# Gathering the expert inputs of rounds 1 to 7 by products with the selection matrix in place of indirect fetches

## What is computed

```python
hn = rmsnorm(h, g_ffn)
gsel = argmax(hn @ w_rg + b_rg)          # one group of 8 experts for each token
vals, idx = top_k(logits of that group, 2)
for each expert e, for its tokens x:     # 640 pairs of token and expert
    y[token] += weight * ((silu(x @ w_gate[e]) * (x @ w_up[e])) @ w_down[e])
h = h + y;  out = rmsnorm(h, g_final)
```

## Time and profile before

| | before |
|---|---|
| median of 3 runs | 1565.03 us |
| the profiled execution | 1562.23 us |
| its span, first to last instruction | 1560.5 us |
| mean granted TensorE clock | 0.90 |
| PE / PEld busy | 83% / 46% |
| DVE / ACT / POOL busy | 31% / 16% / 6% |
| moved by DMA | 485.52 MB |

### The profile page before, as it was taken

The page is one execution under the profiler, slowest core; times in us unless marked ns, Lnnn a source line. Parts: engine busy times, 40 slices in busy tenths (PEclk is TensorE's granted clock), DMA queues, the critical chain, the costliest instruction groups (busy, mean ns, idle before and its releaser), DMA issues.

```text
span 1560.5 us, 18084 instructions
## 1 busy us (share of the span) xinstructions
PE 1291.7 (83%) x7220; PEld 724.3 (46%) x7220; DVE 477.4 (31%) x1017; ACT 255.0 (16%) x684; POOL 93.6 (6%) x257
## 2 busy tenths in 40 slices
PE   7999999999999998969569668667658758767886
PEld 5667777765578885325125224224214214223232
DVE  4387667233431004313103102202202201211334
ACT  4452332343221111110000000000000000000003
POOL 7800000100010002000000000000000000000000
PEclk9999999999999999879879769869879877887898
DMA  9332233251379653899999999999999999999997
GB/s 216 113 109 88 74 109 103 64 165 55 108 251 389 245 208 114 363 427 428 428 428 427 429 428 429 428 427 427 425 428 426 424 427 418 429 429 421 399 425 314
DMA packets 114181, 485.52 MB, mean 311 GB/s; under 512 B 18325, under 2 KB 86233, under 8 KB 86601
## 3 DMA queue, kind: packets, MB, share of 16 engines
q1 hardware_dynamic: 111496, 475.71, 76.5%
q0 software_dynamic: 2336, 8.94, 1.8%
q10 hardware_dynamic: 288, 0.04, 0.0%
HBM read 477.37 MB, written 10.78 MB: 313 GB/s over the span
## 4 chain that ended last, share of the span: by engine, by line
PE 54%; DMA 41%; DVE 2%; issue 1%; SPq 1%; ACT 1%; POOLq 0%; POOL 0%; ACTq 0%; DVEq 0%
DMA arena<-in_w_up 40%; PE ps L2172 20%; PE ps L2448 12%; PE ps L2236 7%; PE ps L2502 2%; PE ps L2240 2%; PE ps L2107 1%; PE ps L2346 1%; PE ps L2320 1%; PE ps L2042 1%; PE ps L2030 1%; PE ps L2482 1%; SPq L562 1%; DMA arena<-in_x_prompt 1%; PE ps L2094 1%
## 5 line engine op out<-in xcount | busy, mean ns | idle before, releaser
L2448 PE MATMUL ps<-arena 128*32 128x512 f32 x2048 | 320.4, 779 | 204.8 <-DMA arena<-in_w_up 198.2
L2172 PE MATMUL ps<-arena 128*128 128x336 f32 (+1 forms) x1152 | 328.3, 442 | 0.0
L2448 PEld LDWEIGHTS ps<-arena 128*32 128x32 f32 x2048 | 84.7, 138 | 433.5 <-issue 432.8
L2172 PEld LDWEIGHTS ps<-arena 128*128 128x128 f32 x1152 | 215.5, 190 | 95.6 <-issue 3.7
L2502 PE MATMUL ps<-arena 128*32 128x512 f32 x1024 | 146.5, 723 | 20.5 <-DVE arena L1799 20.4
L1787 DVE COPY arena<-ps 128x512 f32<-128x512 f32 x31 | 21.4, 691 | 430.6 <-PE ps L2448 430.6
L1196 ACT ACTIVATE arena<-ps 128x128 f32<-128x128 f32 x32 | 8.8, 276 | 678.6 <-PE ps L2482 678.6
L2236 PE MATMUL ps<-arena 128*128 128x256 f32 x512 | 114.4, 382 | 0.0
L2236 PEld LDWEIGHTS ps<-arena 128*128 128x128 f32 x512 | 96.1, 190 | 14.0 <-issue 1.2
L2502 PEld LDWEIGHTS ps<-arena 128*32 128x32 f32 x1024 | 38.4, 129 | 108.7 <-issue 103.4
L1767 DVE TENSOR_TENSOR arena<-arena,ps 128x1024 f32<-128x1024 f32 (+1 forms) x54 | 65.5, 1218 | 65.4 <-PE ps L2346 50.3
(11 more groups left out here) (405 smaller groups left out, 1005.4 us busy)
## 6 DMA issues: line engine op xcount, KB each, us to landing
arena<-in_w_down SPq DMA_DIRECT2D x61, 2048.0 KB, 22.2
arena<-in_w_gate SPq DMA_DIRECT2D x59, 2048.0 KB, 18.8
arena<-in_w_up SPq DMA_DIRECT2D x59, 2048.0 KB, 23.2
arena<-in_w_in SPq DMA_DIRECT2D x15, 2048.0 KB, 8.9
arena<-in_w_out SPq DMA_DIRECT2D x8, 2048.0 KB, 8.4
arena<-in_w_up SPq DMA_DIRECT2D x10, 1024.0 KB, 15.2
arena<-in_w_gate SPq DMA_DIRECT2D x10, 1024.0 KB, 12.5
arena<-in_w_down SPq DMA_DIRECT2D x6, 1024.0 KB, 19.1
```

What stands on the lines that cost most here:

```text
L2172: mm = te.matmul(o, w, x, start=(k == 0), stop=(k == kt - 1))
L2448: mm = te.matmul(ps[CAP * x:CAP * x + CAP, 0, :], xt[:, 4 * q + at, CAP * i:CAP * i + CAP], (next_first[up] if late and q == 0 else wpiece ...
```

## The change

The fetch of rounds 1 to 7 goes, with what fed it. `gather` now serves these rounds too: each of its four quarters is 12 products (4 column groups x 3 token tiles) into a bank of its own, 2 + i, and the quarters are spread over the experts ahead, each in front of step q of expert i as the two tables give it. `hn` is written by ACT in another order of columns, so that each column group of it is contiguous. `HT` is now made ahead of `x_parts`. The clearing of `xrow` on POOL goes too.

```diff
+GATHER_FIRST = {(2, 2): (0, 1), (3, 0): (2,), (3, 2): (3,)}
+GATHER_AT = {(1, 2): (0,), (2, 0): (1,), (2, 2): (2,), (3, 0): (3,)}
...
@@ gpsimd
-            pool.wait_ge(spread_done, 2)
-            gp.memset(xrow, 0.0).then_inc(xrow_cleared, 1)
-
-            pool.wait_ge(xrow_cleared, 2)
-            for m in range(1, NROUND):
-                pool.wait_ge(row_known, m + 1)
-                pool.wait_ge(rows_loaded, 16 * m)
-                pool.wait_ge(x_turned, 4 * m)
-                pool.indirect_dma_start(out=xrow, out_offset=None, in_=hn_rows,
...
@@ scalar
-                sc.activation(hn[0:TR[t], t, :], hrow[0:TR[t], t, :], ACT.Copy, scale=tok[0:TR[t], t, 1:2])\
-                  .then_inc(hn_ready, 1)
+                sc.activation(hn[0:TR[t], t, :].rearrange("r (k p) -> r p k", k=KT),
+                              hrow[0:TR[t], t, :].rearrange("r (p k) -> r p k", k=KT), ACT.Copy,
+                              scale=tok[0:TR[t], t, 1:2]).then_inc(hn_ready, 1)
...
@@ vector: expert
                 if back:
-                    if ahead is not None:
-                        name_row(ahead)
                     add_part(m - 1, 0)
...
-                if i and inputs is not None:
-                    x_parts(inputs)
                 dve.wait_ge(silu_ready, n + 1)
                 ve.tensor_tensor(HT, Hs, gate_up(i)[:, :, 1, :], ALU.mult)\
                     .then_inc(hid_ready, 1)
+                if i and inputs is not None:
+                    x_parts(inputs)
...
@@ tensor
-            def gather(m):
+            def gather(m, quarters, added):
 
                 pe.wait_ge(p_ready, 3 * (m + 1))
                 pe.wait_ge(hn_ready, 3)
-                pe.wait_ge(xT_a, 2 * m)
-                pe.wait_ge(xT_b, 2 * m)
...
+                if added is None:
+                    pe.wait_ge(spread_copied, 2)
+                else:
+                    pe.wait_ge(sc_added, 6 * added)
+                for i in quarters:
                     for k in range(4):
+                        at = 128 * (4 * i + k)
                         for t in range(3):
-                            mm = te.matmul(ps[:, 2 + i % 2, SLOTS * k:SLOTS * (k + 1)], hn[0:TR[t], t, 4 * i + k:D:KT],
+                            mm = te.matmul(ps[:, 2 + i, SLOTS * k:SLOTS * (k + 1)], hn[0:TR[t], t, at:at + 128],
                                            Psel[0:TR[t], t, :], start=(t == 0), stop=(t == 2))
                     mm.then_inc(x_turned, 1)
...
                 for q in range(4):
                     if start:
                         pe.wait_ge((xT_a, xT_b)[q % 2], q // 2 + 1)
+                    if inputs is not None and first and (i, q) in GATHER_FIRST:
+                        gather(inputs, GATHER_FIRST[i, q], None)
+                    elif inputs is not None and not first and (i, q) in GATHER_AT:
+                        gather(inputs, GATHER_AT[i, q], m)
...
                     if back and q == 1:
-                        if ahead is not None:
-                            name_rows(ahead)
                         add_back(m - 1, 0)
-                        if ahead is not None:
-                            pe.wait_ge(row_known, ahead + 1)
                         add_back(m - 1, 1)
...
                 if back:
                     add_back(m - 1, 2)
                     add_back(m - 1, 3)
-                elif i and inputs is not None:
-                    turn_rows(inputs)
```

More of the change, by code:

```diff
@@ L208, in build @@
         Wh, Wsel = r.take(2, TO), r.take(TO)
-        row_scale, tok = r.take(128), r.take(3, 2)
+        r.take(128)
+        tok = r.take(3, 2)
         r = Region(arena, at_c, 8 * TO)
@@ L1768, in add_part, with expert @@
                     .then_inc(last_added if last else sc_added, 1)
-            def expert(m, i, inputs, ahead=None, sel=None, column=slotp, ending=False):
+            def expert(m, i, inputs, sel=None, column=slotp, ending=False):
                 n, first = EPR * m + i, isinstance(m, int) and m == 0
@@ L1848, in x_parts @@
                     dve.wait_ge(x_turned, 4 * m + i + 1)
-                    ve.tensor_tensor(to[:, 4 * i:4 * i + 4], ps[:, 2 + i % 2, :].rearrange("p (k t) -> p k t", k=4),
+                    ve.tensor_tensor(to[:, 4 * i:4 * i + 4], ps[:, 2 + (i % 2 if first else i), :].rearrange("p (k t) -> p k t", k=4),
                                      bc(gT[:, 4 * i:4 * i + 4].unsqueeze(2), 2, SLOTS), ALU.mult)\
@@ L1863, in select @@
                                             op0=ALU.is_equal, op1=ALU.add).then_inc(p_ready, 1)
-            expert(0, 0, 0, None, 1)
-            expert(0, 1, None, 1)
+            expert(0, 0, 0, 1)
+            expert(0, 1, None)
             expert(0, 2, None)
-            expert(0, 3, 1, None, 2)
+            expert(0, 3, 1, 2)
             dve.wait_ge(hn_ready, 3)
@@ L1871, in _ @@
             with dve.Fori(1, NROUND - 1) as m:
-                expert(m, 0, None, m + 1)
+                expert(m, 0, None)
                 expert(m, 1, None)
                 expert(m, 2, None)
-                expert(m, 3, m + 1, None, m + 2)
+                expert(m, 3, m + 1, m + 2)
             dve.wait_ge(whalf, NROUND - 1)
@@ L1880, in _ @@
                 with dve.Fori(0, NOP) as o:
-                    expert(o + (NROUND - 1), 0, o + NROUND, None, o + (NROUND + 1))
+                    expert(o + (NROUND - 1), 0, o + NROUND, o + (NROUND + 1))
                     for i in range(1, EPR):
@@ L1898, in _ @@
             dve.wait_ge(rconst, 2)
-            expert(m_last, 0, None, None, None, slotq)
+            expert(m_last, 0, None, None, slotq)
             dve.wait_ge(wsel_ready, m_last + 1)
@@ L1913, in _ @@
                                         op0=ALU.is_equal, op1=ALU.add).then_inc(p_ready, 1)
-            expert(m_last, 2, None, None, None, slotp, True)
+            expert(m_last, 2, None, None, slotp, True)
             n = EPR * m_last + (EPR - 1)
@@ L1919, in _ @@
             last_norm(0)
-            dve.wait_ge(rows_named, NROUND + 1)
+            dve.wait_ge(rows_named, 2)
             ve.tensor_copy(wq, ps[:, 1, 1:2]).then_inc(wq_ready, 1)
@@ L2294, in name_first_rows, with turn_rows @@
                 stay_busy(6)
[L2296 to L2307, removed]
+            def turn_rows(quarters):
                 for i in quarters:
-                    if first:
-                        pe.wait_ge(rows_scaled, i + 1)
+                    pe.wait_ge(rows_scaled, i + 1)
                     if i == 2:
-                        pe.wait_ge(xT_a, 2 * m + 1)
+                        pe.wait_ge(xT_a, 1)
                     if i == 3:
-                        pe.wait_ge(xT_b, 2 * m + 1)
+                        pe.wait_ge(xT_b, 1)
                     for k in range(4):
[L2316 to L2320, removed]
+                        mm = te.transpose(ps[:, 2 + i % 2, SLOTS * k:SLOTS * (k + 1)], xrow0[:, 4 * i + k:D:KT], ident)
                     mm.then_inc(x_turned, 1)
@@ L2409, in spread_gains, with expert @@
                               start=True, stop=True).then_inc(gains_spread, 1)
-            def expert(m, i, inputs, ahead=None, turned=None, over=False, ending=False):
+            def expert(m, i, inputs, turned=None, over=False, ending=False):
                 n, first = EPR * m + i, isinstance(m, int) and m == 0
@@ L2421, in expert @@
                     name_first_rows()
-                    turn_rows(0, range(2))
+                    turn_rows(range(2))
                 else:
                     if over and i == 0:
-                        gather(rows)
+                        gather(rows, range(4), m - 1)
                     pe.wait_ge(xT_a, 2 * rows + 2)
@@ L2454, in expert @@
                     if start and q < 2:
-                        turn_rows(0, range(2 + q, 3 + q))
+                        turn_rows(range(2 + q, 3 + q))
                     if back and q == 1:
-                        if ahead is not None:
-                            name_rows(ahead)
                         add_back(m - 1, 0)
-                        if ahead is not None:
-                            pe.wait_ge(row_known, ahead + 1)
                         add_back(m - 1, 1)
@@ L2507, in expert @@
                     spread()
-                    name_rows(ahead)
             expert(0, 0, 0)
-            expert(0, 1, None, 1)
-            expert(0, 2, None)
+            expert(0, 1, None)
+            expert(0, 2, 1)
             expert(0, 3, 1)
@@ L2516, in _ @@
             with pe.Fori(1, NROUND - 1) as m:
-                expert(m, 0, None, m + 1)
-                expert(m, 1, None)
-                expert(m, 2, None)
+                expert(m, 0, None)
+                expert(m, 1, m + 1)
+                expert(m, 2, m + 1)
                 expert(m, 3, m + 1)
@@ L2523, in _ @@
                     for i in range(EPR):
-                        expert(o + (NROUND - 1), i, None, None, o + NROUND, True)
```

(3 more changed lines are left out.)

7 lines of the change are left out of this document (removed).

## The result

| | before | after |
|---|---|---|
| median of the runs | 1563.60 us (1561.61 to 1566.14, 5 runs) | 1554.68 us (1552.31 to 1557.71, 5 runs) |
| profiled execution, its span | 1562.23, 1560.5 | 1554.68, 1552.9 |

The ratio is 0.9944, with a 95% interval of 0.9932 to 0.9956: 8.9 us faster (6.9 to 10.6 by the interval), where 19.0 were forecast.

A forecast was written before the change was run, and what follows sets the result against it. DMA, at its ceiling of about 428 GB/s, was taken as the bound. Gains of 17.5 us (fetches) and 1.5 us (round 7), 19.0 in sum, took the median from 1565.0 to 1546.0 us; range 1541 to 1556.

The forecast's parts named there:

- (1): Fetches of rounds 1 to 7: removing them frees 2.5 us of DMA time each, 17.5 us (10.7 to 18.2).
- Rival B: Fetches: only their bytes count, the extra microsecond each stays; gain 10.7 + 1.5, so 1552.8 us; chance 0.12.
- The guess beside the term: Fetches: time beyond their bytes would fit rows spread unevenly over DMA engines; 2.5 against 1.5 us each.
- (2): PE in each round: quarters of 4.2 us replace old work; 96.9 us busy against DMA's 117.5, all hidden.
- Rival D: PE becomes the bound at 10.9 us per quarter: 70 us slower, some 1635 us; chance 0.06.
- C: PE's longer loop stalls on code at jumps back: up to 12 us, 1558, more likely 1552; chance 0.05.
- the four queued loads cover 19 us: Expert 2 in the rounds: PE comes 1.6 us late, which 19 us of queued loads cover.
- (4): Remaining effects, including round 0's strided `hn` write and reload pushed back 8 to 14 us: priced at nothing.
- my bounds for a quarter: Gather quarter on PE: 2.7 us low, 5.4 at the strided turn's pace, 10.9 at half the clock.
- (3): Expert 3's shorter chain, PE 3 to 6 us earlier: 1.5 us back in round 7 (0 to 2.05).
- The 23 us behind the last load stay: Kernel's end: the time from 1537.77 to 1560.5 us was taken as unchanged.

The follow-up runs named there:

- e6: Kernel before with every indirect fetch of rounds 1 to 7 made twice: 1580.33 us, ratio 1.0111.
- e3: Kernel before without the indirect fetches of rounds 1 to 7, PE multiplying zeros there: 1547.84 us, ratio 0.9896.
- e5: Kernel before with each indirect fetch of rounds 1 to 7 replaced by a plain DMA of 80 rows: 1574.81 us, ratio 1.0075.
- e2: Kernel after with ACT writing `hn` in order and PE reading it with the stride: 1551.41 us, ratio 0.9921.
- e1: Kernel after with round 0's gather moved from expert 2 to expert 3: 1546.13 us, ratio 0.9890.
- e4: Kernel after with six idle products on PE ahead of the wait for `hn` in round 0: 1545.80 us, ratio 0.9884.
- e8: e4 with six more idle products ahead of quarter 2 in each of rounds 1 to 6: 1548.58 us, ratio 0.9906.

## Why the prediction was half right

**(1), the seven fetches at 17.5 us: right.** The intervals are level, e6 measures 2.4 and e3 2.2 to 2.5 per fetch. Rival B, bytes only, falls. The guess beside the term, rows spread unevenly over the engines, is what the packet records fit. By the Trainium skill ("DMA: Bandwidth & Descriptors", the section on the SWDGE path) the term was an estimate of 10.6 us; the runs are against it, and e5 more so.

**(2), PE's work hidden: right in the rounds.** A quarter takes 4.30 us (forecast 4.2), as the timeline of after has it:

```profile
877.48 4.30 PE L2265 MATMUL ps<-arena 128*128 128x128 f32 x24
```

PE's waits for weights fell to 121.8 us in 42 from 177.8 in 43. Rival D falls, and e2 shows that even 7.0 us would have been hidden. C falls too: no stand at the jumps of the longer loop shows in the starts. That agrees with the 2048 instructions of the Trainium skill ("Runtime: NRT & Kernel Launch", on instruction fetch) and not with its window of two pages. Expert 2, put at 28.5 us of PE work, held 24.9, at a granted clock of 0.87 where before stood at 0.7. One sentence of this step was wrong, though, and it is the one the next step leaned on: "the four queued loads cover 19 us".

**(4), "the rest, at nothing": this is the step that failed, by 8.5 us.** It saw the place (the first two quarters in round 0), the cause (ACT's stride, "perhaps double", 11.1 measured) and the reload that is pushed back, and priced it at nothing since the queue there "is full too". Two sizes were off:

- The lateness: "8 to 14 us", measured 19. Against e1, where nothing stands between the steps, PE spends 6.03 + 15.03 + 5.70 = 26.8 us from the end of steps q = 0, 1 to the end of q = 2, 3, instead of 3.54 + 5.34 = 8.9. The quarters alone at 8.4 and ACT's wait gave my 14; half clock in the quarters added 6.5, in steps q = 2, 3 another 2.1 over e4; the wait of 3.5 us that PE had there anyway goes off. The price of half the clock stood in my bounds for a quarter, and I carried it to the rounds and not to this place.
- The cover: "19 us", in truth 11 to 13. SP issues w_gate at 690.88 and w_up at 691.31 behind the same step, so of the four loads ahead of w_up one is late with it. The row of before at 672.24 said so, had I read it: 25.51 us to landing, less two loads of 4.9 for the late pair, less 2.46 for the fetch that goes, leaves 13.2 us. The runs agree: 10.2 us late (682.39, e4) costs nothing, 12.9 late (685.09, e8) leaves 3.0 us of DMA dry. 427 GB/s in slice 18 told the rate of the queue, not its depth.

19 less 13 is 6 us, and the windows lacked 8.5; traffic is back only in the window behind the reload at 691.31, and after entered this stretch some 2 us earlier than before (its w_down loads at 648.36 instead of 650.53), so its queue also ended earlier. Sum: 17.5 - 8.5 = 9.0 against 8.9 measured; that the two agree to 0.1 us is luck, by the interval of 6.9 to 10.6 and by what follows.

**(3), the 1.5 us of round 7: it came out at 0.3, and the end cost 1.4.** Expert 3's chain came out as forecast (under 4 us from step 3 to w_down), and the dip behind the loop's exit is gone. The windows of after there:

```profile
1448.00:1452.00 4.00, 4.00 (x13) 1.23 (x17) 1.69 (x3) 0.28 (x1) 0.00 (x0) 1.00 1.00 426
1452.00:1456.00 4.00, 3.35 (x32) 0.78 (x24) 2.90 (x4) 0.50 (x1) 0.00 (x0) 1.00 1.02 434
```

Yet 1429.11 to 1459.90 is 30.79 us, 1.4 over the pace, and the end got longer. The step of before at 1418.20, the last one ahead of round 7, is this one in after:

```profile
1409.48 5.27 PE L2419 MATMUL ps<-arena 128*32 128x512 f32 x32 [4.75 <-DMA arena<-in_w_up]
```

It comes 8.72 us earlier. The last products of steps q in before and, in the second fence, in after:

```profile
1537.77 1.92 PE L2448 MATMUL ps<-arena 128*32 128x512 f32 x16 [1.53 <-DMA arena<-in_w_up]
```

```profile
1528.78 3.62 PE L2419 MATMUL ps<-arena 128*32 128x512 f32 x16 [3.04 <-DMA arena<-in_w_up]
```

The last load lands 8.99 us earlier, so round 7 gave 0.27 us of the 1.5: it takes 119.30 instead of 119.57 us, and most of the 2.05 above four experts is still paid, without the dip that the step took for its cause. And the span is only 7.6 shorter: behind it 24.1 us pass instead of 22.7, since PE, which waited 3.04 instead of 1.53 us, does this step at half the clock. "The 23 us behind the last load stay" was wrong by 1.4 us, in e1 as well (1520.75 to 1544.9). The 30.79 us I can't explain: DMA stands at 416 to 442 GB/s all through it, so nothing is dry, and e1 has such an interval one expert earlier (1391.66 to 1422.57, 30.91). No run was made for it.

## What to carry to other kernels

When a reload is pushed back, work out the cover at its own place: time from issue to landing, less every load that the same step releases, less what the change takes out of the queue; a full GB/s row says nothing of it. Look first at the start of a steady stretch, where the queue is still being built and a change made for the steady rounds lands on an engine that has just waited. Where an engine has to wait ahead of work that gates a queue, putting the work later costs nothing, and keeping PE busy can pay even with products of no use. A transfer that is spread unevenly over the DMA engines is worth what its fullest engine carries, as far as the packet records here tell, and not its mean in bytes.

## What the runs showed of the hardware

- The granted clock fell to 0.50 both when PE had waited 6.03 us (after) and, in e2, when it had waited 0.72 us and was busy with products whose weights are read with a stride (window 668 to 672: 0.65, then 0.50). In the rounds of e2 such products also ran at 1.00 (window 876 to 880). With the wait filled by six products and weights in order (e4) it stayed at 1.00. So a long wait isn't needed for the fall, and the stride doesn't always bring it; what decides stays open.
- A write of 128 x 2048 float32 by ACT with a stride takes 11.10 / 3 = 3.7 us, in order 1.93 us.
- Twelve products of 128 x 128 take 4.30 us with weights in order and 6.98 us with weights read with a stride of 16 elements, at granted clocks of 1.00 and 0.94.
- Under a full queue, 0.66 MB on POOL's queue cost 2.4 us as an indirect transfer and 4.2 us as a plain one, against 1.5 by bytes. Eight row packets of 309 ns on the fullest engine, 2.47 us, fit the indirect price (inferred).
